# A cross attention's norm, context copies and output product reordered in a two-block transformer kernel

## The reference

```python
x = layer_norm(a * x + memory_cross_attention(x, mem, xa_wq[i], xa_wkv[i], xa_wo[i]), ln_g[i, 2], ln_b[i, 2])
x = layer_norm(a * x + 0.5 * swiglu_ffn(x, ffn_w_in[i, 1], ffn_w_out[i, 1]), ln_g[i, 3], ln_b[i, 3])
...
h_c = rms_norm(ctx, norm1_w[0]) * (1.0 + mod_c[1]) + mod_c[0]     # needs only ctx and the conditioning
```

## Time and profile before

| | |
|---|---|
| time, median of 3 runs | 2714.54 us (2710.27 to 2716.71) |
| profiled execution | span 2712.6 us; the page gives no other time for it |
| PE busy | 2477.5 us, 91% |
| DVE busy | 1459.2 us, 54% |
| ACT busy | 503.5 us, 19% |
| transfers | 712.30 MB, mean 263 GB/s |

### The profile page before, as it was taken

The page is one execution under the profiler, slowest core; times in us unless marked ns, Lnnn a source line. Parts: engine busy times, 40 slices in busy tenths (PEclk is TensorE's granted clock), DMA queues, the critical chain, the costliest instruction groups (busy, mean ns, idle before and its releaser), DMA issues. The chain is left out here.

```text
span 2712.6 us, 37104 instructions
## 1 busy us (share of the span) xinstructions
PE 2477.5 (91%) x14598; PEld 1707.6 (63%) x14598; DVE 1459.2 (54%) x2343; ACT 503.5 (19%) x945; POOL 124.4 (5%) x134
## 2 busy tenths in 40 slices
PE   8999999999999979999999799999998987777786
PEld 8997768999999668997676333333334773333233
DVE  7768536776876558767888722232234552112113
ACT  0004414100100231003331111111110541111111
POOL 1000000000000001003221100000000000000000
PEclk9999999999999999999999999999999998888989
DMA  7668542656456456552224899999996329999997
GB/s 239 245 224 293 184 163 81 207 186 201 164 186 217 151 201 228 186 188 78 62 62 163 310 421 422 422 422 422 422 422 270 125 95 409 422 422 422 422 422 322
DMA packets 234434, 712.30 MB, mean 263 GB/s; under 512 B 12677, under 2 KB 134549, under 8 KB 178912
## 3 DMA queue, kind: packets, MB, share of 16 engines
q1 hardware_dynamic: 223328, 675.85, 64.8%
q0 software_dynamic: 9856, 32.16, 3.6%
q10 hardware_dynamic: 1152, 2.93, 0.3%
HBM read 708.69 MB, written 2.20 MB: 262 GB/s over the span
## 5 line engine op out<-in xcount | busy, mean ns | idle before, releaser
L863 PE MATMUL work<-ring,scratch 128*64 128x512 f32 (+1 forms) x3008 | 552.4, 636 | 112.7 <-DMA ring<-in_moe_up 74.2
L863 PE MATMUL work<-rows_h_parts,ring_parts 128*128 128x256 f32 x3072 | 549.7, 285 | 11.2 <-ACT rows_h_parts L1769 6.6
L863 PEld LDWEIGHTS work<-rows_h_parts,ring_parts 128*128 128x128 f32 x3072 | 477.0, 194 | 14.9 <-issue 9.8
L863 PEld LDWEIGHTS work<-ring,scratch 128*64 128x64 f32 (+1 forms) x3008 | 144.6, 126 | 496.2 <-issue 278.7
L863 PE MATMUL work<-cols_x_parts,ring_parts 128*128 128x256 f32 x1536 | 414.9, 286 | 0.0
L2207 DVE TENSOR_TENSOR ring_parts<-ring,ring_parts 128x2048 fp32r<-128x2048 f32 x132 | 302.6, 2292 | 4.5
L863 PEld LDWEIGHTS work<-cols_x_parts,ring_parts 128*128 128x128 f32 x1536 | 287.8, 195 | 1.5
L863 PE MATMUL acc<-ring_parts,rows_h_parts 128*128 128x512 f32 x960 | 279.8, 391 | 0.0
L2822 DVE COPY scratch<-work 128x512 f32<-128x512 f32 x32 | 22.1, 692 | 373.4 <-PE work L863 373.4
L863 PE MATMUL work<-scratch 128*128 128x256 f32 (+4 forms) x1040 | 197.2, 377 | 6.5 <-issue 4.2
L863 PEld LDWEIGHTS acc<-ring_parts,rows_h_parts 128*128 128x128 f32 x960 | 177.0, 188 | 35.8 <-issue 1.0
(11 more groups left out here) (314 smaller groups left out, 2893.2 us busy)
## 6 DMA issues: line engine op xcount, KB each, us to landing
ring<-in_moe_down SPq DMA_DIRECT2D x128, 1024.0 KB, 25.9
ring<-in_moe_up SPq DMA_DIRECT2D x127, 1024.0 KB, 26.6
ring<-in_moe_gate SPq DMA_DIRECT2D x121, 1024.0 KB, 25.4
ring<-in_ffn_w_in SPq DMA_DIRECT2D x88, 1024.0 KB, 7.5
ring<-in_ada_w SPq DMA_DIRECT2D x48, 1024.0 KB, 9.7
ring<-in_ffn_w_out SPq DMA_DIRECT2D x44, 1024.0 KB, 6.8
ring<-in_xa_wkv SPq DMA_DIRECT2D x16, 1024.0 KB, 6.9
ring<-in_da_w_qkv SPq DMA_DIRECT2D x12, 1024.0 KB, 7.0
```

The source lines that it names most:

```text
L863: ins = nc.tensor.matmul(o, lhsT, rhs, start=start, stop=stop, **kw)
```

## The change

On VectorE the second cross attention no longer splits ffn 3's first weight before its layer norm; that split is then done by ffn 3's own `split_first(i, 1)`. The first cross attention is as before. On ScalarE both context tiles are copied first, then both roots of `xa_norm1` follow, then the copy of ada 2. On TensorE the order of the four banks of the output product becomes an entry of a table; for `xa_out1` it is by column halves ((0,0), (1,0), (0,1), (1,1) as (j, cb)), for the others tile by tile as before. `layer_norm` waits for the count of finished banks that its bank has in that order.

```diff
+TILE_BY_TILE = [(j, cb) for j in range(NT) for cb in range(2)]
+HALF_BY_HALF = [(j, cb) for cb in range(2) for j in range(NT)]
+OUT_ORDER = {"da_out": TILE_BY_TILE, "xa_out0": TILE_BY_TILE, "xa_out1": HALF_BY_HALF, "sw_out": TILE_BY_TILE}
...
-                for j in range(NT):
-                    if at.acc:
+                for j, cb in OUT_ORDER[stage]:
+                    if at.acc and cb == 0:
                         pe.wait_ge(acc_read, NT * at.acc - NT + j + 1)
                     c = slice(j * P, (j + 1) * P)
-                    for cb in range(2):
-                        for wp, xp in SPLIT_ORDER:
+                    for wp, xp in SPLIT_ORDER:
...
             for j in range(NT):
                 norm_root("ctx_norm", j, NT + j)
-            cols_from_rows(col_tile("ctx_norm", 0, 0), NT * P)
-            norm_root("xa_norm1", 0, 0)
-            cols_from_rows(col_tile("ctx_norm", 1, 0), (NT + 1) * P)
+            for j in range(NT):
+                cols_from_rows(col_tile("ctx_norm", j, 0), (NT + j) * P)
+            for j in range(NT):
+                norm_root("xa_norm1", j, j)
             ada_out(2)
-            norm_root("xa_norm1", 1, 1)
             for j in range(NT):
                 split_cols("xa_norm1", j)
...
-                            dve.wait_ge(acc_full, 2 * (NT * use + j) + h + 1)
+                            dve.wait_ge(acc_full, 2 * NT * use + OUT_ORDER.get(acc_stage, TILE_BY_TILE).index((j, h)) + 1)
...
                 if i == 1:
                     dve.wait_ge(ctx_landed, 16)
                     mod_norm("ctx_norm", [1], dst=lambda i: rows_h[:, i - NT, :])
-                split_first(2 * i + 1, 1)
+                if i == 0:
+                    split_first(1, 1)
                 layer_norm(f"xa_norm{i}", f"xa_out{i}", ALPHA, LN_EPS)
```

More of the change, by code:

```diff
@@ new lines, in out_product_split @@
+                    for wp, xp in SPLIT_ORDER:
+                        if cb == 0 and xp:
+                            for piece in range(2):
+                                read_out(pe, plan[x_stage].tiles + 2 * j + piece)
+                        elif cb == 0 and not wp:
+                            high_done(x_stage, j)
+                        for half in range(2):
+                            n = at.loads + 2 * (2 * cb + half)
+                            if wp:
+                                split_done(stage, 2 * cb + half)
+                            else:
+                                weight_high_done(n)
+                            ws = parts(n, 4)
+                            for k in range(4):
+                                kk = 4 * half + k
+                                fin = bool(wp and kk == KB - 1)
+                                mm(acc[:, 2 * j + cb, :], xs[xp][:, kk, c], ws[wp][:, k, :],
+                                   kk == 0 and not wp and not xp, fin, acc_full if fin else None,
+                                   done=2 * int(bool(wp and j == NT - 1 and k == 3)))
```

## The result

The changed kernel takes 2699.93 us (median of 4 runs, 2695.52 to 2700.82) against 2715.6 (4 runs, 2710.27 to 2716.71): ratio 0.9941, 95% interval 0.9927 to 0.9955, so 12.2 to 19.8 us faster. The forecast was 2698.3, range 2692 to 2706. In two more sets of runs it was at 0.9937 (0.9924 to 0.9951) and 0.9945 (0.9932 to 0.9959). The profiled execution took 2699.69 us, with a span of 2697.9; by its span it is 14.7 us shorter than the one of before.

What follows compares the result with a forecast made beforehand. The prediction took one chain of VectorE, ScalarE and TensorE waits between the second cross attention and ffn 3 as the bound. Edits 1 and 2 together gave -16.2 us, edit 3 and the clock 0: 2698.3 us, range 2692 to 2706.

Steps and rivals of the forecast that it cites:

- rival 1: TensorE's clock falls once more in the wait for the second split: gain 13.2 us, 2701.3 us; chance 0.17.
- The chain: VectorE's norm starts at 996.8 without the 12.78 us wait; a new 2.0 us root wait, the 3.57 us one gone.
- Rival 3: Something hidden under the 12.78 us wait holds VectorE's norm: gain under 5 us, 2710 to 2714 us; chance 0.05.
- Ada under the norm: TensorE runs ada 2 from 1003.2 to 1010.1, 6.9 us at 2.4 GHz throughout.
- Rival 2: Ada becomes the bound, 13.8 us at half clock: gain 11.8 us, 2702.8 us; chance 0.09.
- The split at full price: VectorE's first weight split of ffn 3, behind the norm, hidden by nothing: 3.47 us, ready at 1015.0.
- TensorE's start at 1015.0: TensorE waits 1.8 us for the first split, then starts ffn 3 at 1015.0; sign: a wait of 1 to 3 us.
- The second group: ffn 3's second group of 24 matmuls starts at 1020.9 instead of 1037.14, behind the second split: 16.2 us earlier.
- Edit 3 at 0: Output product by column halves: first ffn slot lands 0 to 4.4 us earlier, but 1009.4 is in time: gain 0.
- The clock: Low clock before ffn 3 taken as in before, cost 0; never falling is at most 0.3 us better.
- The bound of a second fall: Clock falls again during a wait for the split; 6 us of dense matmuls at half speed: 3.0 us worse.
- Rival 4: Expert stages lose more than the gain: 2.1% slower cancels 16.2 us, 3% gives 2721 us; chance 0.03.

Runs made afterwards that it cites:

- Edits 1 and 3: Each undone alone in the changed kernel: without edit 1, 2707.03 us, 0.9976 of before; without edit 3, 2699.05 us, 0.9940.
- Edit 2: Both context tiles copied, then both roots, ahead of ScalarE's copy of ada 2; alone against the kernel before: 2713.15 us, 0.9996.
- edit 3: Output product by column halves; alone against the kernel before: 2709.11 us, 0.9981.
- edit 1: VectorE's norm ahead of the split of ffn 3's first weight; alone against the kernel before: 2704.1 us, 0.9960.
- edits 1 and 2: The changed kernel with the output product tile by tile again: 2699.05 us, 0.9940 of the kernel before.
- early-start kernel: Changed kernel plus two casts on ScalarE, low parts of x before the subtractions, ffn 3's first matmuls on high parts alone: 2697.06 us, 0.9935 of before.

## Why the prediction was right

- **What the totals can tell.** Their interval, 12.2 to 19.8 us, holds the forecast of 16.2 and also rival 1's 13.2. It is the trace that tells them apart.
- **The chain.** Edits 1 and 3 were each undone alone and cost what their place says. Edit 2 was not undone with edit 3 in place; without edit 3 it is worth 1.9 us of stage on top of edit 1 (26.83 against 24.98). The norm started at 996.68 (forecast 996.8), tile 0's reciprocal came at 1002.76 (1003.1) after a wait of 1.72 (2.0), tile 1's at 1009.00 (1009.3), the small copy at 1011.02 (1011.3). Rival 3 fell with the norm's start.
- **Ada under the norm.** 1003.00 to 1010.01 at a granted clock of 1.00; forecast 1003.2 to 1010.1. Rival 2 fell.
- **The split at full price.** The step was right and its size too small: 4.28 us (1011.26 to 1015.54) instead of 3.47. The copy of ada now ends (1010.80) just before VectorE begins the cast (1011.26), POOL's addition starts behind it (1010.94), and the cast takes 2.03 instead of 1.22. In before the same addition had hit a small operation (1.10 us instead of 0.22), and the sum did not carry it over.
- **TensorE's start at 1015.0** was wrong: 1016.48. Of the 1.5 us, 0.5 are the longer split, and 0.9 a wait that the step left out: ffn 3's first tile needs the work buffer of the first turned piece, which VectorE gives back with its first low part, and that stands behind the split. In before ScalarE's copy was later than both, so the row could not show it. TensorE's wait was 4.40 us in all and not the 1 to 3 that the prediction names as its sign. In the first profile the late start cost nothing, since the second group still waited 0.56 us for the second split. In the other two (and with edits 1 and 2) the first group took the full 5.26 us and the second followed it with no wait, 0.3 us behind the split.
- **The second group** started at 1021.53, forecast 1020.9, for the cast's 0.8 us; the stage gave 15.7 us (15.5 in the other two profiles) where 16.2 were forecast.
- **Edit 3 at 0**: right, 0.0 to 0.2 us. What the prediction did not say is how much of its gain is taken by edit 1: alone it has 5.2.
- **The clock.** The low stretch before ffn 3 was there as taken (0.80, 0.50 and 0.85 in the three 2 us windows from 1015 to 1021), and once, so rival 1 did not come in this kernel. It cost nothing in the first profile and some 0.3 us in the other two, where it held until 1022 and the first group, not the second split, was the bound. That the prediction put it at 0 held by a margin of half a microsecond. The bound of a second fall was right in kind: two variants have the clock low under the second group. The rule of the Trainium skill (page "TensorE: Matmul & The Clock Gate", section "HAM oscillation — how this bites in real kernels") agrees with the traces so far as the falls come where short bursts and waits alternate; that a burst behind each wait starts slow is not what they show, since the changed kernel's first profile has a slow burst behind the wait of 4.40 us and a fast one behind that of 0.56. The waits in that section's case are longer than the 1.8 and 2.5 us to which the prediction applied it.
- **After the stage** the shift is constant to the last layer norm (184.6 us from the first silu in each profile). By the profiled spans the gain is 14.7 us, 1.0 less than the stage's, by the medians 15.7. Between the two profiled executions the Hyena stretch takes 0.8 us off the gain, the first expert stage gives 0.7 back and the second takes 0.9. Rival 4 fell, since each expert stage took the same within 1 us in the two profiles.

## What to carry to other kernels

When several waits follow each other on one chain, an edit's worth is not the wait it removes but how far the next late thing is behind: here a wait of 12.8 us was worth 13.6 when removed alone and 6.8 after two others, and an earlier transfer 5.2 or nothing. Before moving work behind a norm, list for the first instruction of the next stage all it waits for, buffers given back included, and not only its operands. When a wait is gone, look again at what ended last: here it was VectorE's split in one profile and TensorE's own low clock in two others of the same kernel. Where effects are under 0.2%, compare the edited stage between two instructions in the trace, and the total only to see that nothing else moved.

## What the runs showed of the hardware

A POOL addition on SBUF (128x512, 1.27 us alone) and a VectorE instruction on SBUF get in each other's way. In twelve of the thirteen profiles one VectorE instruction that meets it is longer by 0.8 to 1.0 us: the small operation 1.10 or 1.03 instead of 0.22, the cast 2.03 to 2.06 instead of 1.22, the subtraction 3.18 to 3.27 instead of 2.29. Where the subtraction met a held-back addition, the addition itself took 2.10 and 2.11. In the early-start kernel the addition fell on the low parts of x, which read PSUM, and these kept their 2.48 us for four; a 128x1 copy inside the addition kept its 0.15 (changed kernel, 1011.02).

The ends of these rows look like one engine standing still until the other is done, not like both at a lower rate. In five profiles the small operation ends 0.01 to 0.02 us after the addition (in before 1028.44 and 1028.42). In the changed kernel the cast ends 1.08 us after the addition, a little less than its 1.22 alone. With the addition held back it starts at 1020.09 under a cast that ends at 1021.05, and ends 1.1 us after that cast; the subtraction then ends 2.2 us after the addition. No run varies the overlap to test this reading.

TensorE's granted clock fell at the end of a wait of only 1.95 us behind 24 matmuls at full clock, after a thin stretch. Two kernels whose TensorE starts ffn 3 alike (12.9 and 18.4 us behind the context turns) had it at 0.73 and 0.50, and at 1.00 and 1.00, in the same two windows of their one profile each. One kernel in the same place of Hyena had it at 0.89 in two profiles and at 1.00 in a third.
